# Centring the retention values on VectorE instead of in the matmul, and attention's weighted values in bank 5 (PSUM)

## The chip, the cores and the metric

The kernel runs on one core of one Trainium2 chip. The core has TensorE (PE, matmuls into PSUM), VectorE (DVE), ScalarE (ACT), GpSimd (POOL) and SyncE (SP, which issues the loads). Each engine works through its own instruction stream in order, and they meet only at semaphores. The metric is the device time of one execution in microseconds. It is given as the median of the runs, and lower is better.

## The reference

A streaming encoder trunk of two layers, d_model 1024, 512 tokens. Each layer has one wide input projection, three groups of heads side by side (sliding-window attention, retention, state-space), one output projection, and a gated feed-forward part with a short convolution. Retention is the part that matters here:

```python
scores = einsum('bclhd,bcshd->bchls', qc, kc) * decay_in
y_in = einsum('bchls,bcshe->bclhe', scores, vc)
...                                   # y_cross: the state of earlier chunks, also linear in vc
y = y_in + y_cross
mu = mean(y, axis=-1, keepdims=True)  # over the 128 values of a head
var = mean(square(y - mu), axis=-1, keepdims=True)
yn = (y - mu) * rsqrt(var + EPS) * gn_g
```

Since y is linear in the values, the mean can be taken out of the values vc of every token and head beforehand. Both kernels do that. Attention's part is a softmax over 128 keys and `out = einsum('bchgqk,bckhd->bcqhgd', p, vb)`, the weighted values.

## The kernel before

Activations lie with features on the 128 partitions and the 512 tokens along the free axis. A dense projection is cut into units of 128 output features. Each weight tile is split into a high and a low part (`w_hi` by ScalarE at L481, `w_lo` by GpSimd at L378), and a unit of eight weight tiles is 24 matmuls of 512 columns into one of two banks, `dense[0]` and `dense[1]`. VectorE evacuates a unit at L796. The work of the heads uses six more banks, `M[0]` to `M[5]` (`mix` in the trace).

The order is written out by hand in `SCHEDULE`, a list of step names. Every engine walks through the same list and does its own share of each step. `D18` is dense unit 18. The steps of interest are:

- `RV0` to `RV3`: the retention values of one head (units D16 to D19, which lie in `pad`) are brought into token order. PE multiplies each of four 128x128 blocks by `center`, the identity minus 1/128, with the block as the stationary operand. The result in bank 5 is transposed and has zero mean. ScalarE copies it to `vtok` (L596).
- `AS0` to `AS3`: attention logits in banks 0 and 1, scaled and biased by VectorE (L910), the maximum (L920) and its subtraction (L926), then the exponential on ScalarE (L584).
- `AX0` to `AX3`: sum, reciprocal and product on VectorE (L931 to L934). `AT0` to `AT3`: the weights are transposed on PE (L1274) and copied by ScalarE to `pt` (L588).
- `AV0` to `AV3`: the weighted values, in bank 0. ScalarE rounds them to `m_hi`, VectorE subtracts to `m_lo` (L943) and so frees the bank.
- `D20` to `D23` are gate units of the state-space part. ScalarE applies silu (L525) after it has made the next weight tiles' `w_hi`, and VectorE multiplies the product in (L804).

The stretch of the list round the change is this:

```python
"SB2 SA3 D16 D17 SB3 AS0 RV0 D18 RV1 AX0 D19 RV2 AT0 AS1 D20 RV3 AX1 AV0 D21 AT1 AS2 D22 AX2 AV1 "
"SN0 D23 SX0 AT2 AS3 D24 AX3 AV2 SN1 D25 SX1 D26 AT3 RP0 D27 AV3 RP1 D28 RP2 D29 RP3 D30 RA0 D31 "
```

Each bank has a counter of its uses in the order of the list. `BANKS` says which banks a step uses, and `take` makes PE wait on `m_free` until the use before has been released by the engine that read it last. `ready` gives the count. `link` makes VectorE wait for its own last result.

Of the kernel before, what the change touches and what calls it, by code (L numbers as in the profile page):

```python
# [19 lines left out]
D, S, P = 1024, 512, 128  # L20
# [4 lines left out]
BLK = 128  # L25
# [63 lines left out]
def step_of(name):  # L89
# [5 lines left out]

BANKS = {
# [3 lines left out]
}  # L100

# [17 lines left out]


ACT_LINKS = 5
DVE_LINKS = 82


KB = 256
# [45 lines left out]
def build(nc, a, out):  # L171
    f32, f32r = mybir.dt.float32, mybir.dt.float32r
    ALU, ACT, AX = mybir.AluOpType, mybir.ActivationFunctionType, mybir.AxisListType
    with ExitStack() as ctx:
# [19 lines left out]
        rs2 = (ssq, rstd)  # L194
        c_all, p_all = sb("consts", [P, sum(CONSTS.values())]), sb("params", [P, sum(PARAMS.values())])
        consts, par = pieces(c_all, CONSTS), pieces(p_all, PARAMS)
        ident, ones, center, perm = (consts[n] for n in ("ident", "ones", "center", "perm"))
        dvec, sinks = (par[n].rearrange("p (l t) -> p l t", t=4) for n in ("D", "sinks"))
        dt_v, dt_e, dt_u, dt_w, dt_a = (sb(n, [P, 32]) for n in ("dt_v", "dt_e", "dt_u", "dt_w", "dt_a"))
        exp_a = sb("exp_a", [P, 8])  # L200
        bias = sb("bias", [P, 4, P])
        tok = sb("tok", [P, 64])
        lastb, wdec, cdec = sb("lastb", [P, 32]), sb("wdec", [P, 32]), sb("cdec", [P, NB, 4])
        mx, sk, den = sb("mx", [P, 8]), sb("sk", [P, 8]), sb("den", [P, 8])
        scratch = nc.dram_tensor("rel_scratch", (8, 64 * 192), f32, kind="Internal").ap()
        cum_rows = nc.dram_tensor("cum_rows", (8, S), f32, kind="Internal").ap()
# [203 lines left out]
        def _(act):  # L410
# [60 lines left out]
            with act.Fori(0, DEPTH) as l:  # L471
# [28 lines left out]
                for name in SCHEDULE:  # L500
# [58 lines left out]
                    elif step == "BC":  # L559
                        act.wait_ge(m_ready[0], ready(name, 0, l))  # L560
                        nc.scalar.activation(btok, M[0][:, :], ACT.Copy).then_inc(m_free[0], 1)
                    elif step == "SA":
                        for g in range(2):
                            act.wait_ge(l_in, l * 8 + 2 * n + g + 1)
                            lm = lms[:, n % 2, g]
                            nc.scalar.activation(lm, lm, ACT.Exp).then_inc(l_exp, 1)

                    elif step == "SN":
                        act.wait_ge(m_ready[4], ready(name, 0, l))
                        nc.scalar.activation(rs[:, :], M[4][:, :], ACT.Ln, scale=1.0 / 256,  # L570
                                             bias=par["eps"][:, 0:1]).then_inc(m_free[4], 1)
                        act.wait_ge(m_free[4], ready(name, 0, l) + 1)
                        nc.scalar.activation(rs[:, :], rs[:, :], ACT.Exp, scale=-0.5).then_inc(grs, 1)
                    elif step == "SX":
                        for t in (2 * n, 2 * n + 1):
                            act.wait_ge(gn_done, l * 4 + t + 1)
                            split_from(m_hi[:, t, :], xs[:, t, :], s_hi)
                    elif step == "AS":
                        act.wait_ge(m_ready[4], ready(name, 2, l))
                        nc.scalar.activation(vwin[:, n % 2, :, :], M[4][:, 0:2 * P].rearrange(  # L580
                            "p (c d) -> p c d", c=2), ACT.Copy).then_inc(m_free[4], 1)
                        act.wait_ge(lg_in, l * 4 + n + 1)
                        link(nc.scalar.activation(sk[:, :], sk[:, :], ACT.Exp))
                        nc.scalar.activation(lg, lg, ACT.Exp).then_inc(lg_exp, 1)  # L584
                    elif step == "AT":
                        for c in range(2):
                            act.wait_ge(m_ready[2 + c], ready(name, c, l))
                            nc.scalar.activation(pt[:, c, :], M[2 + c][:, :], ACT.Copy).then_inc(m_free[2 + c], 1)  # L588
                    elif step == "AV":
                        act.wait_ge(m_ready[0], ready(name, 0, l))  # L590
                        for c in range(2):
                            src = M[0][:, 256 * c:256 * c + 256].rearrange("p (t q) -> p t q", t=4)
                            split_from(m_hi[:, 4:8, CH * (2 * n + c):CH * (2 * n + c) + CH], src, a_hi)
                    elif step == "RV":
                        act.wait_ge(m_ready[5], ready(name, 0, l))
                        nc.scalar.activation(vtok[:, :, n, :], bank(5, 4), ACT.Copy).then_inc(m_free[5], 1)  # L596
                    elif step == "RB":
                        for j in range(2):
                            act.wait_ge(m_ready[3 + j], ready(name, j, l))
                            dst = ar("ry", 2, 2)[:, :, j, BLK * n:BLK * n + BLK]  # L600
                            nc.scalar.activation(dst, M[3 + j][:, 0:2 * P].rearrange("p (t s) -> p t s", t=2),
                                                 ACT.Copy).then_inc(m_free[3 + j], 1)
                    elif step == "RN":

                        if n == 0:
                            act.wait_ge(m_free[4], ready("RB3", 1, l) + 1)
                            for j in range(2):
                                nc.scalar.activation(sq[:, j, :], ry[:, j, :], ACT.Square).then_inc(r_sq, 1)
                        for j in range(2):
                            act.wait_ge(m_ready[j], ready(name, j, l))  # L610
                            nc.scalar.activation(rs2[j][:, :], M[j][:, :], ACT.Ln, scale=1.0 / P,
                                                 bias=par["eps"][:, 0:1]).then_inc(m_free[j], 1)
                        for j in range(2):
                            act.wait_ge(m_free[j], ready(name, j, l) + 1)
                            nc.scalar.activation(rs2[j][:, :], rs2[j][:, :], ACT.Exp, scale=-0.5)\
                                .then_inc(r_rs, 1)
                        if n == 0:
                            for j in range(2):
                                nc.scalar.activation(sq[:, j, :], ry[:, 2 + j, :], ACT.Square).then_inc(r_sq, 1)
                    elif step == "RX":  # L620
                        act.wait_ge(rn_done, l * 4 + n + 1)
                        split_from(m_hi[:, 8 + n, :], ry[:, n, :], r_hi)
# [39 lines left out]
        def _(dve):  # L662
# [58 lines left out]
            with dve.Fori(0, DEPTH) as l:  # L721
# [30 lines left out]
                for name in SCHEDULE:  # L752
# [183 lines left out]
                    elif step == "AV":  # L936
                        for c in range(2):
                            dve.wait_ge(a_hi, l * 8 + 2 * n + c + 1)
                            at = CH * (2 * n + c)
                            src = M[0][:, 256 * c:256 * c + 256].rearrange("p (t q) -> p t q", t=4)  # L940
                            if c == 0:
                                dve.wait_ge(a_hi, l * 8 + 2 * n + 2)
                            V.tensor_tensor(m_lo[:, 4:8, at:at + CH], src,  # L943
                                            m_hi[:, 4:8, at:at + CH].bitcast(f32), ALU.subtract)\
                                .then_inc(m_free[0] if c else a_lo, 1)
                    elif step == "RP":
                        r = (rk if n < 2 else rq)[:, n % 2, :]

# [95 lines left out]
        def _(pe):  # L1044
# [54 lines left out]
            with pe.Fori(0, DEPTH) as l:  # L1099
# [46 lines left out]
                for name in SCHEDULE:  # L1146
# [6 lines left out]
                    elif step == "D":  # L1153
                        if n < N_IN:
                            dense_unit(n, h_src)
                        else:
                            part = (n - N_IN) // 8
                            if n == N_IN:
                                pe.wait_ge(s_lo, l * 4 + 4)
                            elif n == N_IN + 8:  # L1160
                                pe.wait_ge(m_free[0], ready("AV3", 0, l) + 1)
                            dense_unit(n, m_src(4 * part), ret_tile if n == N_IN + 16 else None)
                    elif step == "NORM":
                        norm(l * 2, name, l)
# [111 lines left out]
                    elif step == "AV":  # L1276
                        take(name, 0, l)
                        for c in range(2):

                            pe.wait_ge(m_free[2 + c], ready(f"AT{n}", c, l) + 1)  # L1280
                            for g in range(2):
                                r = slice(64 * g, 64 * g + 64)
                                ins = mm(M[0][r, 256 * c:256 * c + 256], vwin[:, n % 2, c, r],
                                         pt[:, c, 256 * g:256 * g + 256])
                        ins.then_inc(m_ready[0], 1)
                    elif step == "RP":
                        r = (rk if n < 2 else rq)[:, n % 2, :]
                        pe.wait_ge(evac, l * N_EV + U_RK + n + 1)
# [2 lines left out]
                    elif step == "RV":  # L1291
                        pe.wait_ge(evac, l * N_EV + U_RV + n + 1)
                        take(name, 0, l)
                        for b in range(NB):
                            at = 3 + BLK * b
                            ins = mm(M[5][:, P * b:P * b + P], pad[:, (U_RV + n) % 2, at:at + BLK], center[:, :])
                        ins.then_inc(m_ready[5], 1)
                    elif step == "RA":
                        pe.wait_ge(rot_done, l * 4 + 4)
# [76 lines left out]

CONSTS = {"ident": P, "ones": P, "center": P, "perm": P, "sel": 8, "causal": P, "cos": S, "sin": S,
          "decin": 4 * P, "qdec": 2 * P, "kdec": 4, "gch": 2}  # L1380
PARAMS = {"g": (2 * DEPTH + 1) * KD, "sconv": DEPTH * 30, "sng": DEPTH * 4, "gng": DEPTH * 4,
          "fconv": DEPTH * FT * 4, "D": DEPTH * 4, "sinks": DEPTH * 4, "dtb": DEPTH * 8, "alog": DEPTH * 8, "eps": 1}
# [20 lines left out]
def constants():  # L1403

    import numpy as np
    f = np.float32
    c = {"ident": np.eye(P, dtype=f), "ones": np.ones((P, P), f),
         "center": (np.eye(P) - 1.0 / P).astype(f)}
    perm = np.zeros((P, P), f)
    for m in range(P):  # L1410
        d = m % 64
# [120 lines left out]
```

## Time and profile before

| | us |
|---|---|
| median of 3 runs | 1305.99 (1304.16 to 1306.04) |
| profiled execution, time | 1307.44 |
| its span, first to last instruction | 1305.6 |
| TensorE busy | 1277.4 (98%) |
| VectorE, ScalarE, GpSimd busy | 615.3, 565.3, 588.8 |
| mean granted TensorE clock | 0.996 of full speed |

All times of the trace are counted from the span's start. Layer 0's head part lies between 30 and 265 us, that of layer 1 between 670 and 905 us. A busy share says little here, since PE is busy nearly throughout. What has to be read is the timeline of the engines that PE waits for. Matmuls overlap in the pipeline, so a duration of 0.39 us for 512 columns goes with starts 0.23 us apart.

### The profile page before, as it was taken

How to read it: one execution, taken by the hardware profiler on the slowest of the kernel's cores; microseconds unless marked ns; L12 is line 12 of the kernel's file. 1: busy time of each engine (PE TensorE's matmuls, PEld its weight loads, DVE VectorE, ACT ScalarE, POOL GpSimd, SP SyncE). 2: the span in 40 equal slices, each digit the busy share in tenths (PEclk: the TensorE clock that was granted, in tenths of full speed). 3: DMA queues.
4: the chain of work that ended last, by engine and by line, in shares of the span. 5: the costliest groups of instructions: out<-in, count | busy, mean ns of one | idle time of the engine just before them, and what ended most of it. 6: DMA issues, size and time to landing. Idle time of an engine off the chain costs nothing.

```text
span 1305.6 us, 21212 instructions
## 1 busy us (share of the span) xinstructions
PE 1277.4 (98%) x6114; PEld 1032.3 (79%) x6114; DVE 615.3 (47%) x938; ACT 565.3 (43%) x902; POOL 588.8 (45%) x435
## 2 busy tenths in 40 slices
PE   7999999999999999999999999999999999999996
PEld 4888877778888888888878887777888888888885
DVE  6755666474444103332256556755653430133323
ACT  6432483465444223443344327726644332244433
POOL 4533434254444544554444443424455454455541
PEclk9999999999999999999999999999999999999998
DMA  7335212143333333333323432212333333333333
GB/s 221 91 111 137 74 56 74 49 112 90 96 96 96 97 97 97 96 96 90 98 89 89 131 106 73 76 47 67 91 111 98 96 101 97 91 96 97 96 95 113
DMA packets 77483, 125.29 MB, mean 96 GB/s; under 512 B 7752, under 2 KB 20456, under 8 KB 77288
## 3 DMA queue, kind: packets, MB, share of 16 engines
q1 hardware_dynamic: 77416, 124.43, 33.6%
q8 instruction: 38, 0.62, 0.2%
q14 instruction: 29, 0.24, 0.1%
HBM read 121.84 MB, written 2.55 MB: 95 GB/s over the span
## 4 chain that ended last, share of the span: by engine, by line
PE 83%; DVE 8%; ACT 4%; issue 4%; DMA 0%; DVEq 0%; SPq 0%; ACTq 0%
PE dense L1048 76%; PE mix L1048 6%; DVE h_lo L690 1%; ACT w_hi L481 1%; DVE arena L991 1%; DVE ssq L698 1%; DVE arena L739 1%; ACT L525 1%; DVE arena L993 1%; ACT m_hi L498 0%; DMA x<-in_xT 0%; DVE arena L910 0%; ACT pad L525 0%; DVE mx L920 0%; DVE arena L926 0%
## 5 line engine op out<-in xcount | busy, mean ns | idle before, releaser
L378 POOL TENSOR_TENSOR w_lo<-w_raw,w_hi 128x512 fp32r<-128x512 f32 x424 | 580.3, 1384 | 686.8 <-ACT w_hi L481 680.1
L1048 PE MATMUL dense<-h_hi,w_hi 128*128 128x512 f32 x1120 | 445.3, 398 | 3.9 <-DVE h_lo L690 3.0
L1048 PE MATMUL dense<-h_lo,w_hi 128*128 128x512 f32 x1120 | 437.3, 390 | 0.0
L481 ACT ACTIVATE w_hi<-w_raw 128x512 fp32r<-128x512 f32 x422 | 256.3, 627 | 258.4 <-PE dense L1048 242.4
L1048 PE MATMUL dense<-h_hi,w_lo 128*128 128x512 f32 x1120 | 300.5, 389 | 0.0
L1048 PEld LDWEIGHTS dense<-h_hi,w_hi 128*128 128x128 f32 x1120 | 211.0, 188 | 55.3 <-issue 10.0
L1048 PEld LDWEIGHTS dense<-h_lo,w_hi 128*128 128x128 f32 x1120 | 211.0, 188 | 45.2 <-issue 2.7
L1048 PEld LDWEIGHTS dense<-h_hi,w_lo 128*128 128x128 f32 x1120 | 210.4, 188 | 44.4
L1048 PE MATMUL dense<-m_hi,w_hi 128*128 128x512 f32 x544 | 217.3, 400 | 3.2 <-ACT w_hi L481 2.5
L1048 PE MATMUL dense<-m_lo,w_hi 128*128 128x512 f32 x544 | 212.0, 390 | 0.0
L1048 PE MATMUL dense<-m_hi,w_lo 128*128 128x512 f32 x544 | 146.9, 389 | 0.0
L1048 PEld LDWEIGHTS dense<-m_hi,w_hi 128*128 128x128 f32 x544 | 102.1, 188 | 28.9 <-DVE x L787 3.3
L1048 PEld LDWEIGHTS dense<-m_lo,w_hi 128*128 128x128 f32 x544 | 102.1, 188 | 23.0 <-issue 2.4
L1048 PEld LDWEIGHTS dense<-m_hi,w_lo 128*128 128x128 f32 x544 | 102.1, 188 | 21.4
L1029 DVE TENSOR_TENSOR x<-dense,x 128x512 f32<-128x512 f32 x32 | 22.1, 692 | 192.5 <-PE dense L1048 192.5
L1007 DVE TENSOR_TENSOR arena<-dense,rstd 128x512 f32<-128x512 f32 x44 | 30.5, 692 | 93.6 <-PE dense L1048 93.6
L641 ACT ACTIVATE arena<-arena 128x512 f32<-128x512 f32 x44 | 27.9, 634 | 85.9 <-DVE arena L1014 85.9
L1017 DVE TENSOR_TENSOR arena<-dense,rstd 128x512 f32<-128x512 f32 x44 | 30.4, 691 | 71.2 <-PE dense L1048 71.2
L1010 DVE SCALAR_TENSOR_TENSOR arena<-arena,params 128x512 f32<-128x512 f32 x44 | 35.7, 811 | 59.7 <-ACT arena L636 59.7
L1048 PE MATMUL mix<-arena 64*128 64x128 f32 (+4 forms) x696 | 56.6, 297 | 3.7 <-DVE arena L910 3.7
L423 ACT ACTIVATE h_hi<-x,params 128x512 fp32r<-128x512 f32 x39 | 28.3, 725 | 71.1 <-DVE x L1029 59.5
L1048 PEld LDWEIGHTS mix<-arena 128*64 128x64 f32 (+3 forms) x696 | 42.9, 160 | 17.1 <-issue 12.8
(173 smaller groups left out, 958.3 us busy)
## 6 DMA issues: line engine op xcount, KB each, us to landing
w_raw<-in_w SPq DMA_DIRECT2D x428, 256.0 KB, 2.6
arena<-cum_rows SPq DMA_DIRECT2D x8, 512.0 KB, 5.7
x<-in_xT SPq DMA_DIRECT2D x8, 256.0 KB, 6.3
out_y<-arena SPq DMA_DIRECT2D x8, 256.0 KB, 2.1
arena<-exp_rows SPq DMA_DIRECT2D x12, 128.0 KB, 6.4
consts<-in_consts SPq DMA_DIRECT2D x1, 1223.0 KB, 9.2
rel_scratch<-arena SPq DMA_DIRECT2D x1, 382.0 KB
bias<-rel_scratch SPq DMA_DIRECT2D x8, 32.0 KB, 2.5
```

Source lines behind the costliest of these rows:

```text
L378: nc.gpsimd.tensor_tensor(w_lo[:, s, :], w_raw[:, s, :], w_hi[:, s, :].bitcast(f32), ALU.subtract).then_inc(lo_ready, 1)
L423: nc.scalar.activation(h_hi[:, o, :], x[:, o, :], ACT.Copy, scale=gcol(e, o)).then_inc(h_hi_ready, 1)
L481: nc.scalar.activation(w_hi[:, slot, :], w_raw[:, slot, :], ACT.Copy).then_inc(hi_ready, 1)
L525: nc.scalar.activation(zt, zt, ACT.Silu).then_inc(z_silu, 1)
L641: nc.scalar.activation(fs, fy, ACT.Silu).then_inc(f_silu, 1)
L690: V.scalar_tensor_tensor(h_lo[:, o, :], x[:, o, :], gcol(e, o), h_hi[:, o, :].bitcast(f32), ALU.mult, ALU.subtract).then_inc(h_lo_ready, 1)
L698: V.tensor_tensor(ssq[:, :], ssq[:, :], sq[:, o % 2, :], ALU.add).then_inc(ssq_added, 1)
L1007: V.tensor_tensor(fpad[:, 2:2 + S], dense[0][:, :], rstd[:, :], ALU.mult).then_inc(evac, 1)
L1010: ins = V.scalar_tensor_tensor(fy, fpad[:, 1:1 + S], par["fconv"][:, bass.ds(fi * 4 + 1, 1)], fy, ALU.mult, ALU.add)
L1017: V.tensor_tensor(fb, dense[1][:, :], rstd[:, :], ALU.mult).then_inc(evac, 1)
L1029: V.tensor_tensor(x[:, o, :], dense[n % 2][:, :], x[:, o, :], ALU.add).then_inc(evac, 1)
L1048: return T.matmul(dst, lhsT, rhs, start=start, stop=stop)
```

## The change

Three things change together. In RV, PE now transposes each block plainly (an instruction in transpose mode with the identity). VectorE, which had no part in this step, sums each token's 128 values in the bank, multiplies the four sums by 1/128, and subtracts the mean while it copies the bank to `vtok`. ScalarE's copy is gone. AV uses bank 5 where it used bank 0. The matrix `center` leaves the constants, and `DVE_LINKS` grows by the two new self-waits of each of four steps.

```diff
-    "AS": (0, 1, 4), "AT": (2, 3), "AV": (0,), "RP": (4,), "RV": (5,), "SN": (4,),
+    "AS": (0, 1, 4), "AT": (2, 3), "AV": (5,), "RP": (4,), "RV": (5,), "SN": (4,),
...
-DVE_LINKS = 82
+DVE_LINKS = 90
...
+        vmean = sb("vmean", [P, NB])
...
 # ScalarE
-                        act.wait_ge(m_ready[0], ready(name, 0, l))
+                        act.wait_ge(m_ready[5], ready(name, 0, l))
...
-                    elif step == "RV":
-                        act.wait_ge(m_ready[5], ready(name, 0, l))
-                        nc.scalar.activation(vtok[:, :, n, :], bank(5, 4), ACT.Copy).then_inc(m_free[5], 1)
...
 # VectorE
-                                .then_inc(m_free[0] if c else a_lo, 1)
+                                .then_inc(m_free[5] if c else a_lo, 1)
+                    elif step == "RV":
+                        dve.wait_ge(m_ready[5], ready(name, 0, l))
+                        link(V.tensor_reduce(vmean[:, :], bank(5, 4), AX.X, ALU.add))
+                        link(V.tensor_scalar(vmean[:, :], vmean[:, :], 1.0 / P, None, ALU.mult))
+                        V.tensor_tensor(vtok[:, :, n, :], bank(5, 4),
+                                        vmean[:, :].unsqueeze(2).broadcast_to([P, NB, P]),
+                                        ALU.subtract).then_inc(m_free[5], 1)
...
 # TensorE
-                                pe.wait_ge(m_free[0], ready("AV3", 0, l) + 1)
+                                pe.wait_ge(m_free[5], ready("AV3", 0, l) + 1)
...
-                                ins = mm(M[0][r, 256 * c:256 * c + 256], vwin[:, n % 2, c, r],
+                                ins = mm(M[5][r, 256 * c:256 * c + 256], vwin[:, n % 2, c, r],
                                          pt[:, c, 256 * g:256 * g + 256])
-                        ins.then_inc(m_ready[0], 1)
+                        ins.then_inc(m_ready[5], 1)
...
-                            ins = mm(M[5][:, P * b:P * b + P], pad[:, (U_RV + n) % 2, at:at + BLK], center[:, :])
+                            ins = T.transpose(M[5][:, P * b:P * b + P], pad[:, (U_RV + n) % 2, at:at + BLK],
+                                              ident[:, :])
```

The order of the instructions stays, but what they wait for changes, and VectorE gets new ones. This is TensorE's stream from RV3 to AV0, before (`L1280` is a wait of AV0, `mix0_free` the release of bank 0):

```order
L1048 MATMUL mix<-consts,pad 128x128 [waits mix5_free]
L1048 MATMUL mix<-consts,pad 128x128 x3
L1097 REGISTER_ALU
L1280 REGISTER_ALU [waits mix0_free]
L1048 MATMUL mix<-arena 64x256 [waits mix2_free]
```

And after:

```order
L1301 MATMUL mix<-consts,pad 128x128 [waits mix5_free]
L1301 MATMUL mix<-consts,pad 128x128 x3
L1102 REGISTER_ALU
L1285 REGISTER_ALU [waits mix5_free]
L1053 MATMUL mix<-arena 64x256 [waits mix2_free]
```

Behind RV3's blocks AV0 now waits for the release of the bank that RV3 has just filled.

This is VectorE's stream from D20's evacuation to the start of AX1, before (`pad<-dense` is the evacuation, `arena<-arena,pad` the product that waits for ScalarE's silu, `den<-arena` the first operation of AX1):

```order
L796 TENSOR_TENSOR pad<-dense,rstd 128x512 [waits mix5_ready]
L804 TENSOR_TENSOR arena<-arena,pad 128x512 [waits ssd_y_summed,z_silu]
L930 REGISTER_ALU
L931 TENSOR_REDUCE den<-arena 128x8 [waits lg_exp]
```

And after:

```order
L794 TENSOR_TENSOR pad<-dense,rstd 128x512 [waits mix5_ready,run_done]
L802 TENSOR_TENSOR arena<-arena,pad 128x512 [waits ssd_y_summed,z_silu]
L945 REGISTER_ALU
L946 TENSOR_REDUCE vmean<-mix 128x4 [waits mix5_ready]
L669 REGISTER_ALU
L947 TENSOR_SCALAR vmean<-vmean 128x4 [waits vector_chain]
L669 REGISTER_ALU
L948 TENSOR_TENSOR arena<-mix,vmean 128x4x128 [waits vector_chain]
L928 REGISTER_ALU
L929 TENSOR_REDUCE den<-arena 128x8 [waits lg_exp]
```

RV3's three operations stand behind D20's product and ahead of AX1.

## Rows read from the trace of the kernel before

**Rows 1.** Page, part 4 (chain by engine); and who waited: in total, times, longest.

```profile
PE 83%; DVE 8%; ACT 4%; issue 4%; DMA 0%; DVEq 0%; SPq 0%; ACTq 0%
...
PE dense L1048 76%; PE mix L1048 6%; DVE h_lo L690 1%; ACT w_hi L481 1%; DVE arena L991 1%; DVE ssq L698 1%; DVE arena L739 1%; ACT L525 1%; DVE arena L993 1%; ACT m_hi L498 0%; DMA x<-in_xT 0%; DVE arena L910 0%; ACT pad L525 0%; DVE mx L920 0%; DVE arena L926 0%
...
PE mix L1048 <- DVE arena L910: 3.7, 2, 1.8
```

**Rows 2.** Groups of TensorE by line and form: count, busy us, mean ns, idle before.

```profile
L1048 PE MATMUL mix<-consts,pad 128*128 128x128 f32 x64 | 8.5, 275 | 0.0
...
L1274 PE MATMUL mix<-consts,arena 128*128 128x128 f32 x64 | 8.4, 274 | 0.0
```

**Rows 3.** Single lines of VectorE: duration ns min/median/max, first and last start, form.

```profile
L851 DVE TENSOR_TENSOR arena<-mix,wdec x8: 681/682/686, 77.4 to 757.1; 128x512 f32<-128x512 f32 x8
...
L932 DVE TENSOR_TENSOR den<-den,sk x8: 166/394/860, 139.0 to 830.0; 128x8 f32<-128x8 f32 x8
...
L920 DVE TENSOR_REDUCE mx<-arena x8: 1219/1220/1222, 132.0 to 824.6; 128x8 f32<-128x1024 f32 x8
```

**Rows 4.** Timeline, AS0 to AT0: start us, duration us, engine, line, work, idle before.

```profile
133.62 1.22 DVE L926 TENSOR_TENSOR arena<-arena,mx 128x1024 f32<-128x1024 f32 x1
...
136.08 0.58 ACT L596 ACTIVATE arena<-mix 128x512 f32<-128x512 f32 x1
...
136.85 1.05 PE L1048 MATMUL mix<-consts,pad 128*128 128x128 f32 x8
...
137.14 0.69 DVE L796 TENSOR_TENSOR pad<-dense,rstd 128x512 f32<-128x512 f32 x1 [2.31 <-PE dense L1048]
...
137.75 1.21 DVE L931 TENSOR_REDUCE den<-arena 128x8 f32<-128x1024 f32 x1
...
140.10 2.03 DVE L934 TENSOR_TENSOR arena<-arena,den 128x1024 f32<-128x1024 f32 x1
...
144.12 1.04 PE L1274 MATMUL mix<-consts,arena 128*128 128x128 f32 x8
```

**Rows 5.** Timeline from AS1's exponential to RV3's copy, all engines.

```profile
150.71 1.06 ACT L584 ACTIVATE arena<-arena 128x1024 f32<-128x1024 f32 x1
...
151.67 2.18 ACT L481 ACTIVATE w_hi<-w_raw 128x512 fp32r<-128x512 f32 x4
151.93 1.05 PE L1048 MATMUL mix<-consts,pad 128*128 128x128 f32 x8
152.21 0.69 DVE L796 TENSOR_TENSOR pad<-dense,rstd 128x512 f32<-128x512 f32 x1 [1.78 <-PE dense L1048]
...
152.91 1.08 PE L1048 MATMUL mix<-arena 128*64 128x256 f32 x8
...
153.87 1.28 ACT L525 ACT_TABLE_LOAD   x1
...
155.16 0.63 ACT L525 ACTIVATE pad<-pad 128x512 f32<-128x512 f32 x1
...
155.83 0.87 DVE L804 TENSOR_TENSOR arena<-arena,pad 128x512 f32<-128x512 f32 x1 [2.92 <-ACT pad L525]
...
156.62 1.21 DVE L931 TENSOR_REDUCE den<-arena 128x8 f32<-128x1024 f32 x1
...
157.27 0.58 ACT L596 ACTIVATE arena<-mix 128x512 f32<-128x512 f32 x1
```

**Rows 6.** Timeline of a wait; then stretches: busy (count) by engine, granted clock, DMA.

```profile
24.02 1.77 PE L1048 MATMUL mix<-ssq,consts 128*128 128x512 f32 x2 [3.36 <-DVE ssq L698]
...
24.00:26.00 2.00, 1.98 (x3) 0.97 (x4) 1.09 (x2) 0.17 (x1) 2.00 (x2) 0.59 0.43 49
26.00:28.00 2.00, 2.00 (x7) 1.56 (x6) 0.00 (x0) 1.97 (x3) 0.24 (x1) 0.56 0.61 113
```

**Rows 7.** Timeline round AV2.

```profile
182.35 1.07 ACT L588 ACTIVATE arena<-mix 128x512 f32<-128x512 f32 x2
...
184.01 1.28 DVE L910 SCALAR_TENSOR_TENSOR arena<-mix,bias 128x512 f32<-128x512 f32 x2
184.81 1.08 PE L1048 MATMUL mix<-arena 128*64 128x256 f32 x8 [1.84 <-DVE arena L910]
```

More of the change, by code:

```diff
@@ L196, in build @@
         consts, par = pieces(c_all, CONSTS), pieces(p_all, PARAMS)
-        ident, ones, center, perm = (consts[n] for n in ("ident", "ones", "center", "perm"))
+        ident, ones, perm = (consts[n] for n in ("ident", "ones", "perm"))
         dvec, sinks = (par[n].rearrange("p (l t) -> p l t", t=4) for n in ("D", "sinks"))
@@ L589, in _ @@
                     elif step == "AV":
-                        act.wait_ge(m_ready[0], ready(name, 0, l))
+                        act.wait_ge(m_ready[5], ready(name, 0, l))
                         for c in range(2):
-                            src = M[0][:, 256 * c:256 * c + 256].rearrange("p (t q) -> p t q", t=4)
+                            src = M[5][:, 256 * c:256 * c + 256].rearrange("p (t q) -> p t q", t=4)
                             split_from(m_hi[:, 4:8, CH * (2 * n + c):CH * (2 * n + c) + CH], src, a_hi)
-                    elif step == "RV":
-                        act.wait_ge(m_ready[5], ready(name, 0, l))
-                        nc.scalar.activation(vtok[:, :, n, :], bank(5, 4), ACT.Copy).then_inc(m_free[5], 1)
                     elif step == "RB":
@@ L939, in _ @@
                             at = CH * (2 * n + c)
-                            src = M[0][:, 256 * c:256 * c + 256].rearrange("p (t q) -> p t q", t=4)
+                            src = M[5][:, 256 * c:256 * c + 256].rearrange("p (t q) -> p t q", t=4)
                             if c == 0:
@@ L1375, in _ @@
             ins.then_inc(m_ready[5], 1)
-CONSTS = {"ident": P, "ones": P, "center": P, "perm": P, "sel": 8, "causal": P, "cos": S, "sin": S,
+CONSTS = {"ident": P, "ones": P, "perm": P, "sel": 8, "causal": P, "cos": S, "sin": S,
           "decin": 4 * P, "qdec": 2 * P, "kdec": 4, "gch": 2}
@@ L1406, in constants @@
     f = np.float32
-    c = {"ident": np.eye(P, dtype=f), "ones": np.ones((P, P), f),
-         "center": (np.eye(P) - 1.0 / P).astype(f)}
+    c = {"ident": np.eye(P, dtype=f), "ones": np.ones((P, P), f)}
     perm = np.zeros((P, P), f)
```

## The prediction, made before the changed kernel ran

> **What bounds the kernel now.** I read the chain of waits first. TensorE (PE) holds 83% of it, dense matmuls alone 76% [rows 1]. So what PE spends or waits is the time, and another engine counts only where PE waits for it. The view of who waited for whom says where: the largest total is for VectorE's scaling of attention logits, twice, 3.7 us in all [rows 1]. Then I read the timeline round every step the change touches, to see which engine is late there. The layer loop runs the same list twice, so a gain or loss counts twice; I work in layer 0.
>
> **TensorE's own work.** A product of one 128x128 block by the centring matrix is two instructions: 64 records for 32 blocks, 8.5 us busy, 0.133 us each. A transpose is one: 64 records at L1274 for 64 transposes (eight in each of eight AT steps), 8.4 us, 0.131 us each [rows 2]. An RV step thus falls from eight instructions to four, 0.53 us less; eight steps give 4.2 us if every one reaches the end.
>
> **VectorE's new work.** ScalarE loses a copy of 0.58 us per RV. VectorE gets three operations that wait for each other: a sum of 512 columns, about 0.65 us, being a little over half of the 1.22 us that 1024 columns take; a 128x4 scaling; a subtraction from the bank with a broadcast operand, 0.68 us as L851, which has that form [rows 3]. The small one lies between 0.17 and 0.86 us, the ends of L932 on a 128x8 tile [rows 3]; I take 0.17, since it has one tensor operand and not two. With 0.03 us between operations that is **1.6 us**, bounds 1.5 and 2.3.
>
> **RV0 to AT0: half of the gain arrives.** VectorE finishes AS0's subtraction at 134.84, so RV0 is done there at 136.4. PE, 0.5 us ahead, is through D18 at 136.3 and takes bank 5 for RV1 at 136.5, where before it began at 136.85. VectorE evacuates D18 to 137.2, does RV1 to 138.8, and only then AX0, which took 4.4 us (137.75 to 142.13). It ends at 143.2, and AT0 on PE, which needs it, starts at 143.3 and not at 144.12 [rows 4]. Three shorter RV steps would have brought AT0 to 142.5. Of 1.6 us there arrive **0.8**; what is late next is VectorE. Bounds: 0 and 1.6.
>
> **AV0: a new wait.** Attention's weighted values now need bank 5, and on PE the instruction before AV0 is RV3, which fills bank 5. The order listing in the section on the change shows that nothing lies between. Before, AV0 waited for bank 0, long free, and started 0.98 us after RV3 (151.93, 152.91). The bank now comes free when VectorE has subtracted. VectorE runs in order, and ahead of RV3 stands the product of D20, which waits for ScalarE's silu; ScalarE comes to the silu after AS1's exponential, four w_hi copies and a table load. It starts at 155.16, the product at 155.83, and the next VectorE operation at 156.62 [rows 5]. ScalarE's own copy of RV3 was as late before (157.27), and nobody waited for it. All this comes 0.8 us earlier, so RV3's three operations start at 155.8 and end at 157.4; with 0.1 us for the signal AV0 starts at 157.5, against 152.91: **+4.6 us**. This figure already holds the 0.8 us and all that RV3 saves, since PE only waits longer for having been early. Bounds: +4.0 (the whole 1.6 us arrive) and +6.1 (none does, and the scaling takes 0.86). The instructions queued behind AV0 on PE are D21, AT1 and everything after; nothing else can fill the hole. The other engines catch up in it.
>
> **The clock.** PE stands idle there from about 151.8 to 157.5, 5.7 us. In this trace a wait of 3.36 us before 24.02 was followed by granted clocks of 0.59 and 0.56 over two stretches of 2 us [rows 6], so the engine went to its lower level, 1.2 GHz, for most of them: 0.82 + 0.88 = **1.7 us** of full speed lost. I charge the same to AV0 and D21. Bounds: 0, if the clock holds, and 3.4, if twice that stretch is slow. The Trainium skill ("TensorE: Matmul & The Clock Gate", Part 1: The HAM clock gate) says that the array falls to half rate when idle and must be busy again to recover. By that the fall would come at both AV0 waits; without it the sum below would be 3.4 us smaller.
>
> **AV2: a wait goes.** AS3's scaling on VectorE starts at 184.01, behind SSD's normalization; AV2 waited 1.84 us for it, for the same bank 0, and ran at 184.81. In bank 5 it needs only AV1's release and ScalarE's copies of the transposed weights, 182.35 to 183.42 [rows 7]. PE is ready at 182.97; the first copy is done then and the second when the first half of AV2 has run. **-1.8 us**; the bound is -1.3, if it must wait for the end of both copies.
>
> **What is late next after AV2.** PE now runs 1.8 us nearer to ScalarE and VectorE from SN1 to RP3. ScalarE's copies for AV3 and VectorE's release of bank 4 between the RP steps are the close ones. I take **+0.2 us** given back, bounds 0 and the whole 1.8.
>
> **Hidden or nothing.** The centring matrix leaves the constants (64 KB less to load, in a stretch in which PE waits for VectorE's sums). AV1 and AV3 find bank 5 free, as VectorE's share of AV0 and AV2 ends several us before. RB0 needed RV3 finished before too.
>
> **The sum**, per layer: +4.6 + 1.7 - 1.8 + 0.2 = +4.7; for two layers +9.4 us. The profiled execution took 1307.44 us (span 1305.6), so its like after is 1316.8. The runs shown have their median 1.45 us below it, at 1305.99; with the same difference that makes **1315.4**.
>
> **The rivals.**
> - *The clock holds.* Then the sum is 2 x 3.0 = 6.0 us: 1312.0. For it: the wait at 24.02 followed other idle time, and a stretch of dense matmuls stands before this one. Against: this wait is longer than the one that lowered the clock.
> - *The lead doesn't arrive and AV2's gain is given back.* If the transposes cost as much as the products, so that the change does not shorten PE's work, or if AX0 takes the whole lead, AV0 starts at 158.3 (+5.4); if AV3 and the RP steps then hand back 1 us of 1.8, a layer costs 5.4 + 1.7 - 0.8 = 6.3: 1318.6.
> - *Not slower.* One mechanism: VectorE reaches RV3 right after evacuating D20, because silu and product of D20 don't hold it up. Then RV3 is worked off from 152.0 to 153.6, AV0 starts at 153.7 (+0.8), the idle time is under 2 us and the clock holds; with AV2's -1.8 and +0.2 a layer gains 0.8: 1304.4. It decides from an AV0 start of 154.5, where the +1.6 is what AV2 gives back. For it speaks only that ScalarE has one copy fewer to do. Against it: that copy stands behind the silu, and the four copies and the table load ahead of it, 3.4 us, all remain, while the listing has the product ahead of RV3.
>
> **How the numbers follow.** Forecast with the clock's fall 0.60 (1315.4), clock holds 0.18 (1312.0), lead lost and gain given back 0.15 (1318.6), not slower 0.04 (1304.4); 0.03 for what I have not seen, such as a cheap bank release. The cases share the wait at AV0, so nearly all chance lies on one side. The range takes in both neighbours of the forecast: its low end is the wait with the clock holding and the whole lead arriving, 2 x (4.0 - 1.8 + 0.2) = 4.8, 1310.8, rounded outward for the runs' own spread of 1.9 us to 1310; its high end is the third case with 1 us more of low clock in each layer, 1320.6. A measurement tells about 0.2% (2.6 us) from no change, so faster means below 1303.4 and slower above 1308.6: 0.03, 0.06, 0.91.
>
> **What would show it.** In the view of waits, PE would wait for VectorE's subtraction twice, some 5 to 6 us each, before AV0's matmuls, and the 3.7 us for the logits' scaling would be gone. Behind each of these waits the granted clock would stand at 0.5 for some 3 us. RV's records would be 32, at 0.13 us each. AT0 would start 0.8 us earlier against AS0 than now. I am wrong if AV0 follows RV3 within 2 us, if the clock stays at 1.00 there, or if a wait of several us turns up elsewhere, above all before AT0 or RP2.

## The result

The changed kernel takes 1316.74 us (median of 4 runs, 1316.60 to 1319.23) against 1305.86 us before (4 runs, 1304.16 to 1306.04). The ratio is 1.0091, with a 95% interval of 1.0073 to 1.0108. It is 10.9 us slower, where 9.4 were forecast, and 1316.74 lies inside the stated range of 1310 to 1320.6.

This is the page of the profiled execution after (1316.60 us, span 1314.8), parts 1, 2 and 4, and its largest waits of TensorE (in total, times, longest), which answer to [rows 1]:

```profile
PE 1277.8 (97%) x6082; PEld 1030.0 (78%) x6082; DVE 635.4 (48%) x962; ACT 561.0 (43%) x894; POOL 581.7 (44%) x435
...
PEclk9999899999999999999999998999999999999998
...
PE 83%; DVE 8%; ACT 4%; issue 4%; DVEq 0%; DMA 0%; ACTq 0%; SPq 0%
...
PE mix L1053 <- DVE arena L948: 12.2, 2, 6.1
...
PE mix L1053 <- ACT arena L589: 0.6, 2, 0.3
```

The busy shares hardly moved, and the chain's shares by engine are the same to the per cent. The waits tell the story. TensorE now waits 6.1 us, once in each layer, for `L948`, VectorE's subtraction in RV. The 3.7 us for the logits' scaling are gone. Two slices of the clock row have an 8 where there was a 9.

This is the timeline round the first of the two waits, all engines, to be held against [rows 5]:

```profile
148.26 1.06 ACT L585 ACTIVATE arena<-arena 128x1024 f32<-128x1024 f32 x1
...
149.22 2.17 ACT L482 ACTIVATE w_hi<-w_raw 128x512 fp32r<-128x512 f32 x4
149.48 0.60 PE L1301 MATMUL mix<-consts,pad 128*128 128x128 f32 x4
149.68 0.69 DVE L794 TENSOR_TENSOR pad<-dense,rstd 128x512 f32<-128x512 f32 x1 [1.70 <-PE dense L1053]
...
151.41 1.28 ACT L526 ACT_TABLE_LOAD   x1
152.71 0.63 ACT L526 ACTIVATE pad<-pad 128x512 f32<-128x512 f32 x1
153.37 0.81 DVE L802 TENSOR_TENSOR arena<-arena,pad 128x512 f32<-128x512 f32 x1 [3.00 <-ACT pad L526]
154.10 0.68 DVE L946 TENSOR_REDUCE vmean<-mix 128x4 f32<-128x512 f32 x1
...
154.81 0.52 DVE L947 TENSOR_SCALAR vmean<-vmean 128x4 f32<-128x4 f32 x1
155.36 0.69 DVE L948 TENSOR_TENSOR arena<-mix,vmean 128x512 f32<-128x512 f32 x1
...
156.19 1.98 PE L1053 MATMUL mix<-arena 128*64 128x256 f32 x8 [6.11 <-DVE arena L948]
```

RV3 is through TensorE at 150.1. VectorE evacuates D20 and is then idle for 3.0 us, until ScalarE has finished its four copies, the table load and the silu. Only behind the product `L802` does it come to the bank. AV0's eight matmuls take 1.98 us where they took 1.08, since the clock is down. These are stretches of the same trace (length, busy time and count of PE, PE's weight loads, DVE, ACT and POOL, then the granted clock, DMA share and GB/s):

```profile
150.00:153.00 3.00, 0.08 (x1) 0.00 (x0) 0.37 (x1) 2.97 (x5) 3.00 (x3) 1.00 0.17 34
153.00:156.00 3.00, 0.00 (x0) 0.00 (x0) 2.56 (x5) 0.97 (x2) 2.30 (x2) 0.52 0.79 221
156.00:158.00 2.00, 1.81 (x8) 0.79 (x8) 1.90 (x5) 0.00 (x0) 0.00 (x0) 0.50 0.45 145
158.00:160.00 2.00, 2.00 (x7) 1.53 (x6) 1.63 (x3) 0.66 (x2) 0.00 (x0) 0.51 0.00 0
160.00:162.00 2.00, 2.00 (x10) 1.64 (x9) 0.00 (x0) 0.00 (x0) 0.00 (x0) 1.00 0.03 8
```

The clock fell while TensorE was idle, and AV0 and the start of D21 ran at the lower level.

To see where the time goes, the starts of the same steps in layer 0 can be compared. The after trace is 1.44 us ahead at AS0's scaling (128.82 against 130.26), so 1.44 is added to every difference. The lead has nothing to do with the steps compared: it is there at the first matmuls behind the first long wait (22.61 against 24.02), and over the ten traces of this case AS0's scaling starts anywhere from 127.10 to 131.31, in no order that follows the change.

| step (on PE) | before | after | shift | what came in |
|---|---|---|---|---|
| AT0 | 144.12 | 141.61 | -1.07 | three shorter RV steps |
| AV0 | 152.91 | 156.19 | +4.72 | the wait for bank 5: +5.79 |
| AT1 | 159.58 | 164.56 | +6.42 | the low clock: +1.70 |
| AV2 | 184.81 | 187.82 | +4.45 | AV2's old wait gone: -1.97 |
| AV3 | 205.01 | 208.41 | +4.84 | given back: +0.39 |
| RP2 | 209.76 | 213.41 | +5.09 | given back: +0.25 |

A layer costs 5.2 us by the end of the RP steps. The two spans differ by 9.2 us, which with the 1.44 us of the start makes 10.6 for both layers; the second one costs 5.4. The after trace has these rows for the steps of the table (`L932` is the last operation of AX0, `L589` are the copies for AV3):

```profile
139.45 2.04 DVE L932 TENSOR_TENSOR arena<-arena,den 128x1024 f32<-128x1024 f32 x1
...
141.61 1.09 PE L1279 MATMUL mix<-consts,arena 128*128 128x128 f32 x8
...
164.56 1.03 PE L1279 MATMUL mix<-consts,arena 128*128 128x128 f32 x8
...
187.82 1.11 PE L1053 MATMUL mix<-arena 128*64 128x256 f32 x8
...
207.78 1.07 ACT L589 ACTIVATE arena<-mix 128x512 f32<-128x512 f32 x2
...
208.41 1.14 PE L1053 MATMUL mix<-arena 128*64 128x256 f32 x8 [0.30 <-ACT arena L589]
...
213.41 1.12 PE L1053 MATMUL mix<-arena,consts 128*128 128x512 f32 x2
```

AV3 waits 0.30 us for ScalarE's copies of the transposed weights, which it did not do before. This is the first of the places where PE, now nearer to the others, meets them.

### The profile page after: what moved, and what is told of

Read it like the earlier page. It is cut to its first block, busy times and chain, and to the rows that moved or that the text cites. A ratio compares the mean times of both kernels' runs of the same rounds, so it can differ in the third digit from the quotient of the medians.

```text
span 1314.8 us, 21178 instructions
## 1 busy us (share of the span) xinstructions
PE 1277.8 (97%) x6082; PEld 1030.0 (78%) x6082; DVE 635.4 (48%) x962; ACT 561.0 (43%) x894; POOL 581.7 (44%) x435
## 4 chain that ended last, share of the span: by engine, by line
PE 83%; DVE 8%; ACT 4%; issue 4%; DVEq 0%; DMA 0%; ACTq 0%; SPq 0%
PE dense L1053 75%; PE mix L1053 6%; DVE h_lo L688 1%; ACT w_hi L482 1%; DVE ssq L696 1%; ACT m_hi L499 1%; DVE arena L737 1%; ACT L526 1%; DVE mx L918 1%; DVE arena L924 1%; DVE arena L908 1%; ACT L535 0%; ACT L571 0%; DVE arena L998 0%; DVE arena L1044 0%
## 5 line engine op out<-in xcount | busy, mean ns | idle before, releaser
L379 POOL TENSOR_TENSOR w_lo<-w_raw,w_hi 128x512 fp32r<-128x512 f32 x424 | 573.2, 1367 | 703.1 <-ACT w_hi L482 697.7
L1053 PE MATMUL mix<-arena 64*128 64x128 f32 (+4 forms) x696 | 58.6, 304 | 12.8 <-DVE arena L948 12.2
```

Of the source, the lines that this page charges most:

```text
L379: nc.gpsimd.tensor_tensor(w_lo[:, s, :], w_raw[:, s, :], w_hi[:, s, :].bitcast(f32), ALU.subtract).then_inc(lo_ready, 1)
L1053: return T.matmul(dst, lhsT, rhs, start=start, stop=stop)
```

## The experiments

Each kernel was compared with the kernel before, run beside it, whose median was 1305.86 us for the changed kernel, 1304.87 us for e1 to e4 and 1305.67 us for e5 to e8. So a difference to that median says more than the time alone. The ratios are those on record; the quotient of the two medians differs from them by up to 0.001. The last column counts one trace of each kernel from AS0's scaling in layer 0 to the end of the span, against 1175.34 us before. It leaves out the start, where the traces differ by up to 4.2 us for reasons of their own.

| kernel | median us | ratio to before | 95% interval | from AS0 on, us |
|---|---|---|---|---|
| changed kernel | 1316.74 | 1.0091 | 1.0073 to 1.0108 | +10.6 |
| e2: bank 5 alone | 1317.07 | 1.0094 | 1.0078 to 1.0111 | +12.9 |
| e1: centring alone, AV in bank 0 | 1313.07 | 1.0053 | 1.0034 to 1.0072 | +6.9 |
| e5: changed, AV0 in bank 0 | 1309.52 | 1.0033 | 1.0022 to 1.0044 | +3.4 |
| e3: changed, RV3's VectorE work first | 1306.49 | 1.0012 | 1.0002 to 1.0021 | +0.6 |
| e4: changed, matmuls in the wait | 1312.10 | 1.0050 | 1.0033 to 1.0067 | +7.5 |
| e6: before, AV1 to AV3 in bank 5 | 1303.45 | 0.9982 | 0.9973 to 0.9991 | -1.8 |
| e8: plain transposes, no centring | 1304.64 | 0.9998 | 0.9988 to 1.0007 | -1.7 |
| e7: e3 and e5 together | 1301.71 | 0.9971 | 0.9961 to 0.9980 | -4.2 |

### e2: bank 5 alone

The theory was that the bank is what costs, and the rival that it is VectorE's new work. The edit is the bank's part of the change, made to the kernel before:

```diff
-    "AS": (0, 1, 4), "AT": (2, 3), "AV": (0,), "RP": (4,), "RV": (5,), "SN": (4,),
+    "AS": (0, 1, 4), "AT": (2, 3), "AV": (5,), "RP": (4,), "RV": (5,), "SN": (4,),
```

> The kernel before with attention's weighted values in bank 5 and nothing else: RV stays a product by the centring matrix, copied by ScalarE. Theory: AV0 waits for ScalarE's copy of RV3, which in the kernel before ended at 157.9 of a span in which AV0 began at 152.9: +5.1, clock +1.6, AV2 -1.8, given back +0.7, so +5.6 in each layer, 1317 us. Rival (the centring on VectorE is the cause): at most the AV2 gain shows, 1302 to 1306 us.

Measured: 1317.07 us, the figure of the theory and far from the rival's. TensorE waits for ScalarE's copy of RV3, 4.9 us in each layer (waits: in total, times, longest; then the timeline):

```profile
PE mix L1048 <- ACT arena L596: 9.8, 2, 4.9
...
152.00 0.63 ACT L525 ACTIVATE pad<-pad 128x512 f32<-128x512 f32 x1
...
154.04 0.58 ACT L596 ACTIVATE arena<-mix 128x512 f32<-128x512 f32 x1
...
154.74 1.98 PE L1048 MATMUL mix<-arena 128*64 128x256 f32 x8 [4.92 <-ACT arena L596]
```

The whole loss appears without any new work on VectorE. The lateness of the release comes from the silu of D20, whichever engine makes the release.

That the number came out so exactly is in part luck. Against its own before the kernel lost 12.2 us, where the terms of the theory give 11.2. In layer 0, AV0 stands at +5.0 as expected, but AT1 at +7.9: the low clock cost 2.9 us and not 1.6. In the changed kernel 3 us of the low clock passed while TensorE was still idle (the stretch 153 to 156). Here nearly all of it fell on matmuls: the granted clock is 1.00 up to 154 and 0.55, 0.50, 0.50 and 0.74 over the next four stretches of 2 us, with AV0 starting at 154.74. That is why e2 loses no less than the changed kernel, though its wait is 1.2 us shorter.

### e1: the centring alone

The other half: the changed kernel with AV in bank 0, `"AV": (0,)` and its waits and tiles with it.

> The changed kernel with attention's weighted values back in bank 0; RV stays as changed (transposes, centring on VectorE). Theory (the loss is AV0's wait for bank 5): no wait of several us before AV0 and no fall of the clock there. AX1 now stands behind RV3's 1.6 us on VectorE, and it ended at AT1's start before, so AT1 comes about 1 us late in each layer, and AV2's wait of 1.8 us is back: about 1308 us. Rival (VectorE's new work itself is what costs): 1314 to 1317 us, with the waits spread over RV1, AT0 and AT1.

Measured: 1313.07 us. There is no wait before AV0, as the theory said, but the loss expected was 3 us, and it was 7 (by the ratio and the trace) to 8 (by the medians). The expectation was wrong in its size. TensorE waits at AT1:

```profile
153.73 0.86 DVE L802 TENSOR_TENSOR arena<-arena,pad 128x512 f32<-128x512 f32 x1 [2.99 <-ACT pad L526]
154.52 0.68 DVE L946 TENSOR_REDUCE vmean<-mix 128x4 f32<-128x512 f32 x1
...
156.41 1.21 DVE L929 TENSOR_REDUCE den<-arena 128x8 f32<-128x1024 f32 x1
...
158.09 2.12 DVE L932 TENSOR_TENSOR arena<-arena,den 128x1024 f32<-128x1024 f32 x1
...
160.27 1.97 PE L1279 MATMUL mix<-consts,arena 128*128 128x128 f32 x8 [3.14 <-DVE arena L932]
...
160.00:162.00 2.00, 1.73 (x8) 1.57 (x8) 1.47 (x4) 0.49 (x1) 0.00 (x0) 0.54 0.46 131
```

Before, AX1 ended just as AT1 began. With 1.9 us of RV3 ahead of it and 2.12 us instead of 1.23 for its last product (why that one took longer isn't shown), it ends late, while TensorE comes 1.5 us earlier. The expectation held the first of these and not the other two, nor that a wait of 3.1 us lowers the clock again (0.54 in the last row). So the centring on VectorE has a cost of its own. In the changed kernel it is hidden inside AV0's wait, which is why the losses of e1 (7 to 8 us) and e2 (12 us) do not add up to the 10.9 us of both.

### e5: AV0 alone in bank 0

```diff
-    "AV": (5,)
+    "AV0": (0,), "AV": (5,)
```

> The changed kernel with AV0 alone in bank 0; AV1 to AV3 stay in bank 5. Theory (AT1 is held by AX1, which stands behind RV3 on VectorE, as in the run with all of AV in bank 0, where AT1 waited 3.1 us and the clock fell): the same wait at AT1, but AV2 does not wait 1.3 us for AS3 and some 0.7 is given back later: about 1 us less than that run's 1313, 1312 us. Rival (that run's loss came from AV sharing bank 0 with AS): no wait above 1 us at AT1, 1306 us or less.

Measured: 1309.52 us. The wait at AT1 is there, 3.1 us in each layer, so the rival is out. AV2's wait is gone, and the kernel is better than e1 by some 3 us, not 1: 2.6 by the ratios, 3.4 in the traces. There layer 0 gives 1.0 us. Layer 1 gives 2.5, of which 1.4 is the clock, which was down twice as long in e1's second layer (6.8 us against 3.4 us here).

### e3: RV3's work ahead of the product

```diff
                         elif n in U_Z:
                             t = U_Z.index(n)
+                            if t == 0:
+                                center_values(3)    # the three operations of RV3
                             dve.wait_ge(z_silu, l * 4 + t + 1)
```

> The changed kernel with RV3's three VectorE operations issued right behind D20's evacuation, ahead of the product that waits for ScalarE's silu. Theory: AV0 waits about 2 us instead of 6 us and the clock does not fall; AV0 stands at +1.0 against before, AV2 gives -1.8, 0.7 is given back: 1305.7 us. Rival (the position behind the product is not what holds the bank): 1314 to 1317 us, AV0's wait still above 4 us.

Measured: 1306.49 us (10 runs, 1305.01 to 1309.71). That is 1.6 us above its own before, where the theory had 0.2 us below. This one edit of the order still takes 10 us from the changed kernel:

```profile
152.19 0.69 DVE L802 TENSOR_TENSOR pad<-dense,rstd 128x512 f32<-128x512 f32 x1 [1.73 <-PE dense L1059]
...
152.80 0.68 DVE L752 TENSOR_REDUCE vmean<-mix 128x4 f32<-128x512 f32 x1
153.51 0.19 DVE L753 TENSOR_SCALAR vmean<-vmean 128x4 f32<-128x4 f32 x1
153.73 0.69 DVE L754 TENSOR_TENSOR arena<-mix,vmean 128x512 f32<-128x512 f32 x1
...
154.55 1.08 PE L1059 MATMUL mix<-arena 128*64 128x256 f32 x8 [1.96 <-DVE arena L754]
```

The three operations fit into the time in which VectorE waited for the silu. It is the position behind the product that holds the bank. The theory was wrong in one part, that the clock does not fall. It stayed up behind this wait in layer 0 (1.00 in every stretch from 150 to 160), but not in layer 1, where the wait was as long and AT1 came 1.5 us later for it:

```profile
793.53 1.08 PE L1059 MATMUL mix<-arena 128*64 128x256 f32 x8 [1.96 <-DVE arena L754]
...
794.00:796.00 2.00, 2.00 (x10) 1.32 (x7) 1.17 (x2) 1.10 (x3) 2.00 (x2) 0.62 0.58 188
796.00:798.00 2.00, 2.00 (x6) 1.61 (x5) 1.90 (x4) 0.86 (x3) 0.79 (x1) 0.52 0.57 190
```

### e4: matmuls in the wait

```diff
                     elif step == "AV":
+                        if n == 0:
+                            pe.wait_ge(evac, l * N_EV + 20)
+                            for k in range(FILL):      # FILL = 26
+                                mm(dense[1][:, :], h_hi[:, 0, 0:P], h_hi[:, k % KD, :])
                         take(name, 0, l)
```

> The changed kernel with 26 needless matmuls of 512 columns issued between RV3 and AV0 in each layer, into the dense bank that the next unit overwrites: 5.9 us of work at full clock, in a wait of 6.1 us. Theory (idle time lowers the clock behind AV0): AV0 starts at the same time, the granted clock stays at 1.00, and the time falls by 2 x 1.6 to about 1313.5 us. Rival (the low clock costs nothing, or comes for another reason): 1316.7 us or more.

Measured: 1312.10 us, 4.6 us below the changed kernel. Against its own before it lost 7.2 us where the changed kernel lost 10.9, so 3.7 us of that are the edit's, and 3.1 in the traces from AS0 on; 3.2 were expected. TensorE still reaches AV0 when the bank is released, now with 0.27 us of waiting, and the clock stays at 1.00 (stretches as above):

```profile
148.83 6.19 PE L1054 MATMUL dense<-h_hi 128*128 128x512 f32 x26
155.29 1.08 PE L1054 MATMUL mix<-arena 128*64 128x256 f32 x8 [0.27 <-DVE arena L949]
...
156.00:158.00 2.00, 2.00 (x11) 1.42 (x8) 1.90 (x5) 0.66 (x2) 0.00 (x0) 1.00 0.32 117
158.00:160.00 2.00, 2.00 (x10) 1.65 (x9) 0.65 (x2) 0.63 (x1) 0.00 (x0) 1.00 0.00 0
```

26 needless matmuls make the kernel faster. Idle time is what lowers the clock, and the low clock is about a third of the loss, since at 1.7 us in layer 0 and 2.0 in layer 1 (AT1's shift against AV0's, which e4 does not have) it makes 3.7 of 10.9 us. The Trainium skill ("TensorE: Matmul & The Clock Gate", Part 1: The HAM clock gate) says that the array falls to half rate when idle, and this pair of runs agrees: 0.50 behind the idle wait, 1.00 behind the filled one.

### e6: AV1 to AV3 in bank 5, the rest as before

> The kernel before with AV1 to AV3 in bank 5 and AV0 still in bank 0; RV as before. Theory: only AV2's wait of 1.84 us goes, 0.7 comes back at AV3 and between the RP steps, so -1.1 in each layer, 1302.7 us against 1304.9. Rival (PE only meets the next late engine and nothing is gained): 1304 to 1305 us.

Measured: 1303.45 us, faster than before by 0.18% (interval 0.09 to 0.27%), and 2.2 us below its own before, as expected. The wait for the logits' scaling is gone, and the 0.3 us at AV3 has come:

```profile
PE mix L1049 <- ACT arena L588: 0.6, 2, 0.3
```

In its trace AV2 stands 1.9 us earlier against AS0 than before, and the stretch behind the RP steps 1.1 us earlier. So 0.8 us of each 1.9 us are given back, which isolates the term that the prediction held at 0.2.

### e8: TensorE's saving alone

The product by the centring matrix is replaced by a transpose in the kernel before, and ScalarE copies as before. The centring is left out.

> The kernel before with the plain transpose in RV and ScalarE's plain copy: the centring of the values is left out altogether, so the time is that of TensorE's saving alone. Theory: 0.53 us less in each of eight steps, all of it kept up to AT0 and AT1 since VectorE gets nothing new and the chain behind AS1 moves along; -1.6 in each layer, 1301.7 us. Rival (VectorE's AX steps hold PE even without new work): -0.5 in each layer or less, 1304 us.

Measured: 1304.64 us (10 runs), a ratio of 0.9998, 0.9988 to 1.0007. That is no measurable gain, and the expectation of 1.6 us in a layer was wrong. The trace, counted from AS0 on, shows 0.8 us in a layer. The rival was right in kind, but AX is only one of two places. RV1 must wait for ScalarE's copy of RV0, and AT1 for AX1:

```profile
133.25 0.57 ACT L596 ACTIVATE arena<-mix 128x512 f32<-128x512 f32 x1
...
133.88 0.66 PE L1296 MATMUL mix<-consts,pad 128*128 128x128 f32 x4 [0.22 <-ACT arena L596]
...
PE mix L1274 <- DVE arena L934: 0.7, 2, 0.4
```

### e7: both mends

RV3's VectorE work comes first, as in e3, and AV0 is in bank 0, as in e5.

> The changed kernel with RV3's VectorE work ahead of D20's product and AV0 in bank 0. Theory: nothing waits for bank 5, AX1 starts right behind the product as in the kernel before, so the lead of 1.0 us reached at AT0 stays, with under 1 us of waiting at AT1, the clock stays up, and AV2's gain is added: -1.0 - 0.7 to -1.1 in each layer, 1301 us. Rival (AX1 is still too late, so that the clock falls behind AT1): 1305 us or more.

Measured: 1301.71 us (9 runs, 1300.22 to 1303.09), a ratio of 0.9971, 0.9961 to 0.9980, and 4.0 us below its own before, as the theory's -2 in a layer has it. It beats both kernels. Nothing waits for bank 5. AX1 starts right behind the product, and AT1 waits 0.35 us:

```profile
151.92 0.88 DVE L813 TENSOR_TENSOR arena<-arena,pad 128x512 f32<-128x512 f32 x1 [1.42 <-ACT pad L526]
152.72 1.21 DVE L940 TENSOR_REDUCE den<-arena 128x8 f32<-128x1024 f32 x1
...
155.69 1.09 PE L1286 MATMUL mix<-consts,arena 128*128 128x128 f32 x8 [0.35 <-DVE arena L943]
```

The changed kernel's idea is sound. What cost 11 us was one place in VectorE's order and one bank of one step.

## Why the prediction was right

**TensorE's own work.** One transpose is one instruction: there are 32 records now (4.9 us busy, 0.153 us each), and 64 before [rows 2]. But a step does not save the 0.53 us that the instruction counts gave. Against AS0 the dense matmuls behind RV0 start 0.49 us earlier, those behind RV1 another 0.33 us. This term was a little too large; why is not shown.

**VectorE's new work.** The sum takes 0.68 us and the subtraction 0.69 us, where 0.65 and 0.68 were taken from [rows 3]. The scaling takes 0.17 to 0.52 us. RV3, the one that matters, had the slow one, so it took 1.95 us from 154.10 to 156.05 and not 1.6.

**RV0 to AT0.** The forecast was 0.8 us of lead, and 1.07 us arrived. VectorE is what is late there, as argued, but only just. AX0's last product ends at 141.49 and AT0 starts at 141.61, 0.65 us after RV2; in e8, where VectorE has no new work, AT0 follows RV2 after 0.43 us (140.06, 140.49). So about 0.2 us were lost at the meeting point, and not 0.8. TensorE had saved less, and AX0 ran 0.2 us shorter than the 4.4 us taken for it (137.32 to 141.49).

**AV0.** The forecast was +4.6 us, and it is +4.7. So near a hit is luck in part: RV3's operations took 0.35 us more than the 1.6 taken, and what stands ahead of them came 0.27 us earlier than forecast. The mechanism was the one read from [rows 5]: the silu, then the product, then the bank. (The lower bound of +4.0 was worked out wrongly: with the whole lead of 1.6 us instead of 0.8 it is 4.6 - 0.8 = +3.8. The range, rounded outward to 1310, does not change by it.) e2 shows that the bank is enough for it, and e3 that the place behind the product is its cause.

**The clock.** The forecast was 1.7 us, and it is 1.70 in layer 0, and 1.97 in layer 1. That it fits so well is in part luck, since e2 lost 2.9 and 2.6 us in its two layers behind a shorter wait. e4 shows that it is the idle time. The rival in which the clock holds is out for this kernel, though e3 shows that it does happen at a wait of 2 us.

**AV2.** The forecast was -1.8 us, and it is -1.97. The bound of -1.3 was not touched, since the copies for AV2 came in time.

**What is late next.** This is the mis-sized step. The prediction took +0.2 us for it, with bounds of 0 and 1.8, and it is +0.75 (0.39 up to AV3, 0.25 up to RP2, 0.1 behind). e6 has it alone, at 0.8. The close ones were named rightly, ScalarE's copies for AV3 and the RP steps, but no row was laid beside them. ScalarE's chain behind AS3 is busy nearly without a gap and does not move when TensorE does: from AS3's exponential to the copies for AV3 it takes 14.62 us before (188.35 to 202.97), after (193.16 to 207.78) and in e6 (187.18 to 201.80) alike.

**The sum.** It was +4.7 us in a layer, and +5.2 and +5.4 came. Twice the missing 0.6 is the difference between 9.4 and the 10.6 of the profiles. The prediction also put a non-slower case at 1304.4 us, if VectorE worked RV3 off right behind the evacuation. e3 is that case: AV0 stands at +0.6 against before, and the kernel takes 1306.5 us. In its trace, counted from AS0's scaling to the same place in layer 1 and from there to the end, the first part gains 0.35 us and the second loses 0.9; what is given back and the clock's fall in layer 1 make the difference.

## What to carry to other kernels

A bank (or any buffer) handed from one user to the next ties the next user to the release by the engine that reads it, and in an engine that runs in order that release is as late as the latest wait queued ahead of it. So before moving a step to another bank, look up in the timeline when the last reader lets go of it now, even if nobody waits for that yet: here ScalarE's copy at 157.27 was 4.4 us later than the matmuls that were to depend on it. And when PE is made faster or loses a wait, lay the next two meeting points beside it, since in e8 half and in e6 two fifths of the gain ended there.

## What the runs showed of the hardware that was not expected

A wait of TensorE of only 1.96 us was followed by the lower clock once (0.62 and 0.52 over the next 4 us) and by full clock once, in the same execution of e3. The ten runs of that kernel lie between 1305.01 and 1309.71 us, which is wider than the 2 us or so of the kernel before; that the clock's fall in one layer, both or none makes this spread fits its size (1.5 us each), but no run shows it, and the start is a rival for it.

At the start TensorE waits for VectorE's sums in every trace, and the clock behind this wait differs. After waits of 2.46 to 2.98 us (e2, e4, e7, e8) it stayed at 1.00. After waits of 3.13 to 3.39 us it fell, and 1.7 us of full speed were lost before, after and in e1, e5 and e6, and 3.4 us in e3. AS0's scaling starts at 127.1 to 127.8 us in the first four, at 128.8 to 130.3 in the next five, and at 131.3 in e3. It does not follow the edits, since both outcomes come with the centring matrix among the constants and without it. So two executions can differ there by as much as some of the effects measured here, which is why small effects are better read from a step behind it.

VectorE's scaling of a 128x4 tile takes 0.17 to 0.26 us in most places and 0.52 us in RV3 of the changed kernel, while in e3, with GpSimd at work as well, it takes 0.19 us. What makes the difference stays open.
